# Moving a Hyena mixer's last gate into the first steps of an attention loop

## The reference

```python
h = rms_norm(x, norm_mix)
u_hy, q, k, v = split(h @ w_in)              # 3*512, 512, 128, 128 columns
# Hyena: a short convolution, then two long convolutions, each followed by a gate
v_, g1, g2 = split(conv3(u_hy) + short_b)    # 512 channels each
z = v_
for o, gate in enumerate((g1, g2)):
    z = gate * (irfft(rfft(z, 2 * L) * k_f[o])[:L] + skip[o] * z)
# grouped-query attention: 8 query heads, 2 key heads of 64, rotary positions
y_at = softmax(q_ @ k_.T / 8) @ v            # q_, k_ normed per head and rotated
y = concat(group_rms_norm(z), group_rms_norm(y_at))
x = x + y @ w_out
```

## Time and profile before

| | us |
|---|---|
| median of three runs | 782.58 (782.36 to 782.60) |
| the profiled execution | 782.62 |
| its span, first to last instruction | 780.7 |
| TensorE busy (matmuls) | 724.8, 93% of the span |
| VectorE busy | 603.6, 77% |
| ScalarE busy | 474.5, 61% |
| GpSimd busy | 88.4, 11% |

### The profile page before, as it was taken

How to read it: one execution, slowest core, us unless ns; L and a number is a source line. 1 busy time by engine, 2 the same in 40 slices (tenths; PEclk the granted TensorE clock), 3 DMA queues, 4 the chain that set the end, 5 groups by cost and what they waited for, 6 DMA issues and landing times.

```text
span 780.7 us, 10823 instructions
## 1 busy us (share of the span) xinstructions
PE 724.8 (93%) x3634; PEld 601.2 (77%) x3634; DVE 603.6 (77%) x900; ACT 474.5 (61%) x703; POOL 88.4 (11%) x104
## 2 busy tenths in 40 slices
PE   5899999999888688989999998999999999999994
PEld 2666888889777676778786887888888888888882
DVE  5779679997966687553566678999998999998981
ACT  5944140536426878432666342788888888878882
POOL 0000000111100000000000002012322332222111
PEclk9999999999999999999999988999999999999997
DMA  8660111755622000022130974999999999999741
GB/s 289 190 143 28 55 55 54 145 109 121 149 72 108 1 1 1 28 65 97 58 105 10 355 294 154 425 364 377 378 378 377 374 395 372 364 372 380 298 156 22
DMA packets 34038, 150.66 MB, mean 193 GB/s; under 512 B 6063, under 2 KB 9903, under 8 KB 27856
## 3 DMA queue, kind: packets, MB, share of 16 engines
q1 hardware_dynamic: 25584, 134.42, 46.8%
q0 software_dynamic: 8416, 15.74, 9.4%
HBM read 145.94 MB, written 12.58 MB: 203 GB/s over the span
## 4 chain that ended last, share of the span: by engine, by line
PE 77%; ACT 8%; DVE 7%; DMA 4%; issue 2%; SPq 0%; POOL 0%; DVEq 0%; ACTq 0%; POOLq 0%
PE bank L2132 18%; PE bank L2549 11%; PE bank L2551 11%; PE bank L2550 11%; PE bank L2070 9%; PE bank L2077 3%; DMA w_lo<-in_w_in 2%; PE bank L2544 2%; PE bank L2145 1%; PE bank L2488 1%; ACT pr L1062 1%; PE bank L2108 1%; PE bank L2463 1%; PE bank L2462 1%; PE bank L2461 1%
## 5 line engine op out<-in xcount | busy, mean ns | idle before, releaser
L1983 DVE TENSOR_TENSOR e_lo<-slot,e_hi 128x1024 fp32r<-128x1024 f32 x192 | 221.4, 1220 | 8.8 <-ACT e_hi L1112 8.8
L1112 ACT ACTIVATE e_hi<-slot 128x1024 fp32r<-128x1024 f32 x192 | 188.1, 1062 | 6.5 <-PE bank L2551 3.4
L772 ACT ACTIVATE w_hi<-w_raw 128x1024 fp32r<-128x1024 f32 x41 | 42.8, 1055 | 87.7 <-DMA w_raw<-in_w_in 57.6
L2549 PE MATMUL bank<-e_hi,hgT_hi 128*128 128x512 f32 x240 | 95.0, 396 | 0.3 <-DVE hgT_lo L1995 0.3
L2551 PE MATMUL bank<-e_hi,hgT_lo 128*128 128x512 f32 x240 | 93.6, 390 | 0.0
L2550 PE MATMUL bank<-e_lo,hgT_hi 128*128 128x512 f32 x240 | 93.4, 389 | 0.0
L1232 DVE TENSOR_TENSOR w_lo<-w_raw,w_hi 128x1024 fp32r<-128x1024 f32 x31 | 37.6, 1222 | 33.0 <-ACT w_hi L772 32.7
L2549 PEld LDWEIGHTS bank<-e_hi,hgT_hi 128*128 128x128 f32 x240 | 45.3, 189 | 9.5 <-DVE hgT_lo L1995 0.7
L2551 PEld LDWEIGHTS bank<-e_hi,hgT_lo 128*128 128x128 f32 x240 | 45.1, 188 | 9.6
L2550 PEld LDWEIGHTS bank<-e_lo,hgT_hi 128*128 128x128 f32 x240 | 45.1, 188 | 8.9
L2549 PE MATMUL bank<-e_hi,gaT_hi 128*128 128x512 f32 x120 | 48.1, 401 | 0.0
(11 more groups left out here) (422 smaller groups left out, 1718.3 us busy)
## 6 DMA issues: line engine op xcount, KB each, us to landing
slot<-in_w_down SPq DMA_DIRECT2D x16, 2048.0 KB, 15.8
slot<-in_w_gate SPq DMA_DIRECT2D x16, 2048.0 KB, 14.6
slot<-in_w_up SPq DMA_DIRECT2D x16, 2048.0 KB, 14.9
w_raw<-in_w_in SPq DMA_DIRECT2D x18, 512.0 KB, 3.7
w_lo<-in_w_in POOLq DMA_DIRECT2D x10, 512.0 KB, 5.9
w_raw<-in_w_out SPq DMA_DIRECT2D x8, 512.0 KB, 3.9
w_raw<-in_w_k_mem SPq DMA_DIRECT2D x4, 512.0 KB, 6.3
x_in<-in_x SPq DMA_DIRECT2D x4, 512.0 KB, 9.2
```

The source lines that it names most:

```text
L772: act.activation(w_hi[ring(m)][:], w_raw[ring(m)][:], ACT.Copy).then_inc(s_wh, 1)
L1112: act.activation(e_hi[buffer(b, j)][:], slot[slot_][:, 1024 * part:1024 * (part + 1)], ACT.Copy).then_inc(s_ehi, 1)
L1983: dve.tensor_tensor(e_lo[slot_][:, at_], slot[slot_][:, at_], e_hi[buffer(b, j)][:].bitcast(F32), ALU.subtract)\
L2549: pe.matmul(dst, act_hi, w_hi_, start=first, stop=False)
```

## The change

- The gate's four transposes (`gT`) move from ahead of the attention to its steps 1 to 4 (`GATE_STEPS`), the four inverse transforms of the second convolution (two per channel half) to steps 5, 7, 8 and 9 (`INV_STEPS`), each followed one step later by ScalarE's copy or VectorE's product. They use bank 7.
- The norm of the Hyena rows moves back: squares from step 11, root at 17, products from 19; their transposes to steps 23, 25, 27, 28.
- The last spectrum's sums (`filtered(1, 1)`) leave VectorE: GpSimd makes them (`last_product`, `last_first_level`, `last_second_level`), between the DMAs of the last weight pieces. VectorE only multiplies (`multiplied_last`) and takes its other work in another order.
- g2's first piece (22) gets a slot of its own (`extra_piece`), in space that is free after the last forward transform; SP and ScalarE wait for that (`wait_slot`). The pieces behind it move up by one in the ring.
- The 16 filler products go. g2's last piece moves behind the first transposes of keys and queries.
- Several tiles get other places in SBUF (`kT`, `att`, `oT`, `o_sq`, `ident_pair`).

```diff
-HR_STEPS = [17, 20, 24, 28]
-Y_SQUARE_STEP = 2
-Y_ROOT_STEP = 8
-Y_NORM_STEP = 10
+GATE_STEPS = [1, 2, 3, 4]
+INV_STEPS = [5, 7, 8, 9]
+HR_STEPS = [23, 25, 27, 28]
+Y_SQUARE_STEP = 11
+Y_ROOT_STEP = 17
+Y_NORM_STEP = 19
...
+        def wait_slot(eng, n):
+            if n == extra_piece:
+                eng.wait_ge(s_ab, 2)
+                wait_filled(eng, ("fwd", 1, 1, 3))
+            elif ring_turn(n) > 1:
+                wait_used(eng, max(m for m in range(n) if ring(m) == ring(n)))
...
@@ GpSimd
+            def last_product():
+                pool.wait_ge(s_spec, 1)
+                pool.tensor_tensor(x[:, 0:4], products[:, 0:4], products[:, 4:8], ALU.subtract)
+                link(pool.tensor_tensor(x[:, 4:8], low[:, 0:4], low[:, 4:8], ALU.add))
+            def last_first_level():
+                y0, y1, y2, y3 = (pair(x, n, 4) for n in range(4))
+                pool.tensor_tensor(level[2], y1, y3, ALU.add)
+                for w in range(2):
+                    pool.tensor_tensor(first_level[:, 3, (1 - w) * HC:(2 - w) * HC], y1[:, w], y3[:, w], ALU.subtract)
+                pool.tensor_tensor(level[0], y0, y2, ALU.add)
+                link(pool.tensor_tensor(level[1], y0, y2, ALU.subtract))
+            def last_second_level():
+                pool.tensor_tensor(pair(low, 0, 4), level[0], level[2], ALU.add)
...
+            for n in range(ADDED[0], ADDED[-1] - 1):
+                add_piece(n)
+            last_product()
+            add_piece(ADDED[-1] - 1)
+            last_first_level()
+            add_piece(ADDED[-1])
+            last_second_level()
...
@@ ScalarE
             evac_second(("fwd", 1, 1))
+            weight_hi(22, 1)
             head_rms(40, MT * MH, MHD, 1)
...
-            weight_hi(22, 1)
+            weight_hi(23, 2)
...
-            weight_hi(23, 3)
-            act.wait_ge(s_ab, 4)
+            weight_hi(25, 1)
+            head_rms(240, TT * NQ, HD, 2)
+            head_rms(230, TT * NKV, HD, 3)
+            act.activation(small[:, 398:399], eps, ACT.Exp)
+            act.wait_ge(s_spec, 1)
...
+                if s - 1 in GATE_STEPS:
+                    gate_row(1, GATE_STEPS.index(s - 1))
+                if s == TT:
+                    act.wait_ge(s_ab, 4)
...
@@ VectorE
+            spectrum(1, 1)
+            multiplied_last()
             for i in range(TT):
                 wait_freed(dve, ("q", i))
-            roped(0)
-            spectrum(1, 1)
-            made = multiplied(1, 1)
-            filtered(1, 1, made)
-            roped(1)
+            for i in range(TT - 1):
+                roped(i)
...
+            outer_taps(8, 10)
             dve.wait_ge(s_qinv, 1)
             for s in range(AHEAD + 1):
                 gqa_max(s)
...
+            outer_taps(10, 12)
...
+                if s - 1 in INV_STEPS:
+                    gated(1, *divmod(INV_STEPS.index(s - 1), 2))
...
@@ TensorE
             main_chunk("kv")
-            main_chunk("g2")
-            inv_jobs(1, 0)
+            main_chunk("g2", slice(0, 3))
...
-            constant_products(("kT", 0), 16)
             pe.wait_ge(s_klo, 1)
             kT_job(0)
             kT_job(1)
             pe.wait_ge(s_qlo, TT)
             for h in range(2):
                 qT_job(h)
-            gate_jobs(1)
-            inv_jobs(1, 1)
+            main_chunk("g2", slice(3, 4))
...
+                if s in GATE_STEPS:
+                    gate_job(1, GATE_STEPS.index(s))
+                if s in INV_STEPS:
+                    inv_job(1, *divmod(INV_STEPS.index(s), 2))
```

More of the change, by code:

```diff
@@ L104, in psum_jobs @@
     jobs += inverse(0, 0) + gate(0) + inverse(0, 1) + transform("fwd", 1, 0) + transform("fwd", 1, 1)
-    jobs += [("q", i) for i in range(TT)] + [("kv", i) for i in range(TT)] + [("u", c) for c in range(8, 12)]
-    jobs += inverse(1, 0)
-    jobs += [("kT", 0), ("kT", 1), ("qT", 0), ("qT", 1)] + gate(1) + inverse(1, 1)
+    jobs += [("q", i) for i in range(TT)] + [("kv", i) for i in range(TT)]
+    jobs += [("kT", 0), ("kT", 1), ("qT", 0), ("qT", 1)] + [("u", c) for c in range(8, 12)]
     n = TT * NQ
@@ L345, in build @@
                                           "dft", "idft", "x2", "g_moe", "wr", "skip")}
-        ring_ld = [sem(f"ring_ld{s}") for s in range(NSLOT + 1)]
+        ring_ld = [sem(f"ring_ld{s}") for s in range(NSLOT + 2)]
         s_wh = sem("weight_hi_ready")
@@ L349, in build @@
         s_wn = sem("weight_negated")
-        added_ld = [sem(f"weight_added{s}") for s in range(NSLOT)]
+        added_ld = [sem(f"weight_added{s}") for s in range(NSLOT + 2)]
         ring_used = sem("ring_used")
@@ L812, in z_half_hi, with gate_row @@
                     act.activation(quarter(zt_hi, h, rp), quarter(gateT[0], h, rp), ACT.Copy).then_inc(s_zhi, 1)
[L814 to L818, removed]
+            def gate_row(o, r):
+                job = ("gT", o, r)
+                wait_filled(act, job)
+                free(act.activation(gateT[o][:, r, :], bank(job)[:], ACT.Copy), job)
             def dft_parts_hi():
@@ L878, in _ @@
             weight_hi(17, 2)
-            gate_rows(0)
+            for r in range(NR):
+                gate_row(0, r)
             weight_hi(19, 1)
@@ L910, in _ @@
             q_split_hi(1, 2)
-            head_rms(230, TT * NKV, HD, 2)
             q_split_hi(2, 3)
@@ L1355, in butterfly, with outer_taps @@
                 wait_freed(dve, turned)
-            def outer_taps(lo):
-                for c0 in (lo, lo + 2):
+            def outer_taps(lo, hi):
+                for c0 in range(lo, hi, 2):
                     for c in (c0, c0 + 1):
@@ L1555, in _ @@
             spectrum(0, 1)
-            outer_taps(4)
+            outer_taps(4, 8)
             made = multiplied(0, 1)
             filtered(0, 1, made)
-            gated(0, 0)
-            z_half_lo(0)
-            gated(0, 1)
-            z_half_lo(1)
+            for h in range(2):
+                for rp in range(2):
+                    gated(0, h, rp)
+                z_half_lo(h)
             spectrum(1, 0)
@@ L2191, in z_jobs, with gate_job @@
                     transposes(("zT", r), [u[:, c, r:T:NR] for c in range(CT)])
-            def gate_jobs(o):
+            def gate_job(o, r):
                 for c in range(4 * (o + 1), 4 * (o + 2)):
                     wait_freed(pe, ("u", c))
-                for r in range(NR):
-                    transposes(("gT", o, r), [u[:, 4 * (o + 1) + c, r:T:NR] for c in range(CT)])
+                transposes(("gT", o, r), [u[:, 4 * (o + 1) + c, r:T:NR] for c in range(CT)])
             mlp(0)
@@ L2277, in _ @@
             main_chunk("g1", slice(1, 4))
-            inv_jobs(0, 0)
+            for rp in range(2):
+                inv_job(0, 0, rp)
             main_chunk("q", slice(0, 1))
-            gate_jobs(0)
+            for r in range(NR):
+                gate_job(0, r)
             main_chunk("q", slice(1, 2))
-            inv_jobs(0, 1)
+            for rp in range(2):
+                inv_job(0, 1, rp)
             fwd_jobs(1, 0)
```

126 lines of the change are left out of this document (70 added, 56 removed).

## The result

The changed kernel took 776.71 us (median of four runs, 776.32 to 778.78) against 782.59 (782.36 to 782.71): a ratio of 0.9918, 95% interval 0.9895 to 0.9941. So it is 5.9 us faster where 13.9 were forecast. Run once more beside the experiments, the same two kernels gave 778.97 and 782.02, a ratio of 0.9959 (0.9941 to 0.9976). The profiled execution took 778.78 us for a span of 776.9, 3.8 us less than the span of before.

A forecast was written before the change was run, and what follows sets the result against it. The prediction took TensorE, busy nearly throughout, to bound the kernel, with idles and clock falls as leaks. Its terms, -17.7 + 1.0 + 0.7 + 2.1 = -13.9 us, took 782.6 to 768.7 us; range 763 to 776.

The forecast's parts named there:

- to the first score: From the forward transforms to the attention's first score: reached at 224.8 instead of 242.5, 17.7 us earlier.
- attention, to the 12th transpose: Early attention steps: moved gate and inverse transforms mostly fill old idle, plus 0.5 for bank 7; +1.0 us, bounds 0 and 5.
- to the 23rd: Attention steps 10 to 22: exchanged work costs 0, a possible clock fall behind the root 0.7; +0.7 us, bounds -1 and 3.
- to the first output tile: Steps 22 to 29: crowded Hyena row transposes 1.6, clock ahead of the output tiles 0.5; +2.1 us, bounds 0 and 4.
- the 2.9 us of new idle: Ahead of kv: TensorE waits 2.9 us for ScalarE's copy of q, delayed by piece 22, in place of 2.5 removed.
- GpSimd's sums: The last spectrum's sums moved to GpSimd: taken as 13.5 us, between 7.5 and 14.7.
- I put 6: VectorE's delay by GpSimd's sums: 6 us, bounds 0 and 13.5; against 4 of cover, 0.5 on the path.
- the exchange of the rest: Attention steps 10 to 22: two Hyena row transposes leave, root, squares and reductions or products come; net 0.
- The first, VectorE shut out: Rival: each GpSimd sum holds VectorE for its whole time, TensorE waits for the splits; 775.2 us, chance 0.20.
- The second (holes cost nothing): Rival: the clock stays up at kv and later, and shifted ScalarE and VectorE work is hidden; 763.4 us, chance 0.13.
- The third (no idle to fill): Rival: TensorE work moved into the attention finds no idle there and adds its time; 777.6 us, chance 0.07.
- The fourth (bank 7 a relay): Rival: each of eight added bank 7 uses waits a whole attention step; slower, 786.8 us, chance 0.05.

The follow-up runs named there:

- late sums: Against the changed kernel, GpSimd issues all accumulating loads first and begins its sums after VectorE's last split: 776.84 us, again 776.43.
- The move alone: The changed kernel without the extra slot, sums on VectorE, ScalarE's weight copies as before the change; only the new order of work stays: 774.34 us, ratio 0.9897.
- q's copies first: Against the changed kernel, ScalarE copies the extra-slot weight piece behind q's rows instead of ahead of them: 781.69 us, ratio 0.9988.

## Why the prediction was wrong

The sign was right, the size was not. Counted in the profiled executions, term by term:

| term | forecast | measured |
|---|---|---|
| ahead of the forward transforms | 0 | +0.9 |
| to the first score | -17.7 | -11.5 |
| attention, to the 12th transpose | +1.0 | +1.5 |
| to the 23rd | +0.7 | +2.6 |
| to the first output tile | +2.1 | +3.0 |
| behind it | 0 | -0.3 |
| sum | -13.9 | -3.8 |

The attention's stretches are 29.81, 26.73 and 19.85 us before. The profiled execution is the slowest of the four, 2.1 us over their median, so against the medians 8.0 us are missing, not 10.1.

**To the first score, 6.2 us.** By the forecast's own steps: kv at F + 73.7, measured 74.1; the 2.9 us of new idle were 3.22, ended by ScalarE's copy of q, and the clock did fall (14.40 us of matmuls for 11.5, so 2.9 where I had 1.6). g2 came 15.1 us behind kv, not 13.8. The clock alone does not explain that: in the later profile of the changed kernel it stayed up at kv, and TensorE idled until the same moment, F + 89.4:

```profile
202.05 0.47 PE L2196 MATMUL bank<-hT_hi,w_hi_extra 128*128 128x512 f32 x1 [3.72 <-ACT qkv L953]
```

ScalarE set it. I had seen it stand at piece 24 and allowed 0.6 for what is behind; the load was done 1.8 us later against F than I had it (199.84, forecast 197.1). I had given it the 3.60 us of the earlier trace rows. In the later profile it was issued at 192.61 and took 6.69 us, beside GpSimd's accumulating DMA of piece 23 (191.71 to 199.10). In the first, kv's slow matmuls freed its slot late: it was issued at 196.10 and took 3.71. Both landed at F + 86.5 to 86.6. The pieces of g2 then ran as forecast (16.5 for 16.4), and the largest failed step follows.

**GpSimd's sums** I had at 13.5 us; alone they took 15.0 (213.76 to 228.8). That term was close, though the fixed part that I took off the proportion (14.7) does not show in it. What failed is "I put 6" for VectorE's delay: it was 14.1 us of stretch, even over my upper bound of 13.5. The kernel with late sums shows how much of it told: there VectorE idles 3.98 us for kv's rows, the split of the keys ends at 211.87, and TensorE comes for it at 218.08, 6.2 us of cover. In the changed kernel that split ended at 222.41, 10.5 us later, of which 0.9 is the early clock. So 9.6 us of net delay against 6.2 of cover leave 3.4, and the stall is 3.33 us (forecast 0.5), and behind it a fall of the clock, which made the last piece 6.47 us instead of 5.48. My argument that half of the sums would meet reductions and waits was not wrong in kind: the reductions were free. But the two rotations that met the first, long sums each waited one of them out, and the two that met a run of four or five waited to the end of the run. The 0.94 us of the earlier trace rows was a meeting with a single short instruction, and there it was GpSimd that waited, while VectorE kept its 1.22 us (1.23 for that size in the earlier trace rows): no measure of a run of four, nor of which side waits.

**The attention, 3.2 us.** The first part came out as worked out (+1.5 for +1.0): TensorE is busy 29.35 of 31.29 us, so the moved transforms fill the old idle and then bound the steps. The second part failed in size: the stall behind the root is 2.16 us, as put, but I had set the exchange of the rest at 0; with the root's fall of the clock the stretch of the 20th to 23rd transpose alone is 2.2 us longer (9.47 for 7.32). The run without the root shows 2.4 us of that stretch to be the root's, but no gain in the total. The end has its 1.6 and more: 2.56 us ahead of the last transposes, behind a Hyena row's difference on VectorE. No run takes the crowding away without moving the root, so its price in the total stays open.

**The rivals.** The first, VectorE shut out, is what the rows show, and its 775.2 us is near the result; I had given it 0.20, and it should have been the likeliest. That its time is so near is in part luck: it put 6.5 us on top of the forecast for the wait, where the profile has about 4 (3.33 for 0.5, and 1.0 in the last piece), and the attention's 3.2, which it did not hold, filled the rest. By the time alone the third's 777.6 is as near, so only the rows tell them apart. The second (holes cost nothing) is refuted by the windows of that execution: 0.80, 0.87 and 0.94 of the clock behind idle. The third (no idle to fill) is refuted for the early steps; for the later ones it may hold a part. The fourth (bank 7 a relay) is refuted: 0.9 us of idle between the 4th and the 13th probability transpose (27.7 us), where the eight added uses of the bank stand.

**What I didn't see at all:** that the slot, with its copy ahead of q's rows, could be a loss. I set its 2.9 us of idle against 2.5 removed, and counted the second wait (2.4 us and its clock) as its gain. The move alone shows that the new order removes that wait by itself.

## What to carry to other kernels

Work that is given to an idle engine should be checked against what the other engine does in the same microseconds: a VectorE instruction with two SBUF operands paid here for a whole run of GpSimd instructions (6.44 us for 0.69), so put such runs where VectorE waits or reduces, or leave them on VectorE. A copy that waits for a load should not stand in an in-order queue ahead of copies that free a bank: the extra buffer showed its gain only once two such copies stood behind the rows they blocked, and the first of these edits, made alone, was a loss. And when a kernel changes in three ways, run the parts alone: by the later run of the change, one part held more than the whole gain.

## What the runs showed of the hardware

In a run of four GpSimd lost nothing while VectorE waited: its sums began 1.25 us apart beside a held rotation (210.01 to 213.77 for three steps) and as far apart alone (223.79 to 227.54); only the length of each record differed, 1.72 against 1.28. The Trainium skill, "SBUF — State Buffer", section "Who interferes with whom", says that the one that comes later waits while the other's instruction runs. Two long sums agree: the rotation at 193.98 ended behind the first of them (2.83 us), the next behind the second. But the one at 209.60 was held over four, 6.44 us: where records of GpSimd overlap by some 0.5 us (211.28 begins before 210.01 + 1.74), a waiting VectorE instruction did not get in between. Nor was it the one that came later: its record begins 0.41 us ahead of the first of the four sums. The same shows twice with q's copies first (198.66 ahead of a sum at 199.26, 205.44 ahead of 205.92). Why it was held even so, no run here settles; GpSimd's records are rough, and it was issuing a DMA at each of these moments.

The granted clock does not answer the same idle in the same way each time: the two profiles of the changed kernel idled 3.22 and 3.02 us ahead of kv, and the clock of kv was 0.80 in one and 1.00 in the other:

```profile
186.59:202.05 15.46, 11.74 (x97) 11.57 (x97) 15.15 (x16) 7.48 (x14) 6.58 (x4) 1.00 0.69 143
```

Three more profiles idled as long there: 3.12 us with late sums (0.89 over kv and the idle behind it), 3.18 in its second run and 3.19 with the sums on VectorE (1.00 in both). So the clock fell in two of five, and a fall behind an idle of 3 us could be forecast here as a bound, not as a term.
